# The value half of a dense expert layer with tokens as output rows, summed in PSUM over all blocks

## The reference

```python
x = x + peer(rmsnorm(x, g_ffn), ...)           # 128 x 128 experts of one neuron
#   ids, gates: for each token and 8 heads, the 16 best of 128^2 experts
#   act = gelu(h . u[ids]);  out = sum over the chosen of gates * act * v[ids]
ple_gate = sigmoid(rmsnorm(x, g_ple) @ w_ple_gate)
x = x + ple_gate * (p @ w_ple_proj)
return rmsnorm(x, g_final)
```

## Time and profile before

| | |
|---|---|
| median of 3 runs | 1931.49 us (1930.06 to 1932.35) |
| the profiled execution | 1934.96 us, its span 1933.1 us |
| mean granted TensorE clock | 0.983 |
| TensorE busy | 1854.1 us, 96% of the span |
| VectorE, ScalarE, GpSimd busy | 1271.2, 750.4, 1137.2 us |
| DMA | 360.90 MB, 187 GB/s |

### The profile page before, as it was taken

How to read it: one execution, slowest core, us unless ns; L and a number is a source line. 1 busy time by engine, 2 the same in 40 slices (tenths; PEclk the granted TensorE clock), 3 DMA queues, 4 the chain that set the end, 5 groups by cost and what they waited for, 6 DMA issues and landing times.

```text
span 1933.1 us, 24399 instructions
## 1 busy us (share of the span) xinstructions
PE 1854.1 (96%) x9045; PEld 1611.0 (83%) x9045; DVE 1271.2 (66%) x2244; ACT 750.4 (39%) x1190; POOL 1137.2 (59%) x666
## 2 busy tenths in 40 slices
...
GB/s 196 78 66 66 58 99 95 120 67 87 103 140 145 147 131 215 172 180 174 186 192 173 185 172 235 216 166 323 331 328 343 325 347 326 327 335 349 194 33 44
DMA packets 187509, 360.90 MB, mean 187 GB/s; under 512 B 17408, under 2 KB 123904, under 8 KB 185728
## 3 DMA queue, kind: packets, MB, share of 16 engines
...
## 4 chain that ended last, share of the span: by engine, by line
PE 75%; POOL 17%; issue 3%; DMA 2%; DVE 1%; ACT 1%; ACTq 0%; SPq 0%; DVEq 0%
PE bank L745 36%; PE bank L553 11%; PE bank L555 10%; PE bank L554 10%; POOL wl L492 7%; POOL picked L520 6%; PE bank L770 2%; POOL gout L527 2%; POOL rows_h L527 2%; POOL rows_ex L527 1%; DMA raw<-stream 1%; PE bank L649 1%; PE bank L669 1%; PE bank L723 1%; PE bank L639 0%
## 5 line engine op out<-in xcount | busy, mean ns | idle before, releaser
L492 POOL TENSOR_TENSOR wl<-raw,wh 128x1024 fp32r<-128x1024 f32 x298 | 737.9, 2478 | 670.3 <-ACT wh L847 668.7
L847 ACT ACTIVATE wh<-raw 128x1024 fp32r<-128x1024 f32 x338 | 356.5, 1055 | 383.7 <-PE bank L555 195.2
L553 PE MATMUL bank<-hh,wh 128*128 128x512 f32 (+1 forms) x1056 | 396.6, 376 | 30.5 <-DVE x L1400 19.2
L745 PE MATMUL bank<-hh,wh 128*128 128x512 f32 x1024 | 400.3, 391 | 0.8 <-ACT scores L1002 0.8
L745 PE MATMUL bank<-hh,wl 128*128 128x512 f32 x1024 | 400.9, 391 | 0.0
L745 PE MATMUL bank<-hl,wh 128*128 128x512 f32 x1024 | 399.6, 390 | 0.0
L555 PE MATMUL bank<-hh,wl 128*128 128x512 f32 (+1 forms) x1056 | 389.4, 369 | 0.0
L554 PE MATMUL bank<-hl,wh 128*128 128x512 f32 (+1 forms) x1056 | 389.3, 369 | 0.0
L553 PEld LDWEIGHTS bank<-hh,wh 128*128 128x128 f32 x1056 | 202.6, 192 | 60.7 <-DVE x L1400 21.5
L745 PEld LDWEIGHTS bank<-hh,wl 128*128 128x128 f32 x1024 | 192.2, 188 | 37.8
L745 PEld LDWEIGHTS bank<-hl,wh 128*128 128x128 f32 x1024 | 192.3, 188 | 36.9
...
## 6 DMA issues: line engine op xcount, KB each, us to landing
raw<-stream SPq DMA_DIRECT2D x338, 512.0 KB
score_dram<-gout ACTq DMA_DIRECT2D x128, 256.0 KB, 2.5
...
gate<-gate_dram SPq DMA_DIRECT2D x16, 1536.0 KB
score_in<-score_dram SPq DMA_DIRECT2D x128, 192.0 KB
x<-xT SPq DMA_DIRECT2D x4, 512.0 KB, 5.5
picked<-score_dram,score_at POOLq DMA_INDIRECT x128
...
```

Source lines behind the costliest of these rows:

```text
L492: nc.gpsimd.tensor_tensor(wl[:, n % SL, :], raw[:, n % RAW, :], wh[:, n % SL, :].bitcast(F32), ALU.subtract).then_inc(lo_done, 1)
L553: nc.tensor.matmul(out, ah, bh, start=start, stop=False)
L745: last = nc.tensor.matmul(psum[u % 2][:], w(weights, U_DENSE + u, c), tokens[c][:, :], start=c == 0 and which == 0, stop=c == DC - 1 and w ...
L847: nc.scalar.activation(wh[:, n % SL, :], raw[:, n % RAW, :], ACT.Copy).then_inc(hi_done, 1)
```

## The change

In the V stage the activations are stationary (128 tokens of a tile) and V rows move, 512 columns at a time: a block is 3 tiles x 2 halves of the width x 3 matmuls = 18. A unit is one block of V as it lies in DRAM. The sums of all 128 blocks stay in six PSUM banks (`pairs[1]` to `pairs[3]`, a tile each), into which x is turned first (`turn_x`: 8 matmuls with the identity, for tiles 0 to 2 in the last U blocks, for tile 3 in V block 0). `add_values` is gone. Activations lie in a ring of 8 blocks, and gelu works in two PSUM banks. The last 4 blocks are done tile by tile, so that a tile's norm can begin while the next is summed.

The sum of tile 0 begins with the turned x and lies in SBUF (`sparse_sum`), and there are 8 row buffers and a lag of 5 steps. VectorE makes two of three low halves of the V stage. In the closing stage tokens are rows: ScalarE squares a tile with a sum along the row, VectorE scales the identity by 1/rms, and TensorE turns and scales the tile by 8 matmuls with it (`turn_scaled`), twice for each tile. Gate and embeddings have tokens as output rows as well (192 and 48 matmuls of 512 columns); the embeddings are copied out of PSUM. Two gate halves of 4 tiles follow, and the closing norm and the stores go tile by tile. x, hh and hl are now single tensors. The core of the diff (new waits of the closing stage and its last functions are left out):

```diff
@@ -63,16 +62,18 @@
...
-GELU_BANKS = 3
-OUT_BANKS = 3
+LAST = 4
+RING = 8
...
-ROWS = 6
-ROW_LAG = 4
+ROWS = 8
+ROW_LAG = 5
...
-N_UNITS = U_PLE + DC + 2
+U_GATE = U_PLE + 3
+N_UNITS = U_GATE + DC
+END_ORDER = (1, 2, 0, 3)
...
@@ -132,14 +133,9 @@
...
-COPY_STEP = 119
-TURN_STEP = 121
-ADD_STEP = 122
 def low_by_dve(n):
-    return U_V0 + SL <= n < U_PLE and n % 3 == 0
+    return U_V0 + SL <= n < U_PLE and n % 3 != 0
...
@@ -271,34 +269,29 @@
...
+act_h = sb("act_h", [P, RING, DENSE], F32R, ex)
+act_l = sb("act_l", [P, RING, DENSE], F32R, ex)
+sparse_sum = sb("sparse_sum", [P, D], F32, ex)
...
+emb1 = sb("emb1", [P, TT, T], F32, pl)
+squares = sb("squares", [P, D], F32, pl)
...
+emb = [gout, emb1]
+xt = [sparse_sum[:]] + [x[:, 2 * t:2 * t + 2, :].rearrange("p a t -> p (a t)") for t in range(1, TT)]
+pairs = [ctx.enter_context(nc.psum_tensor(f"pair{b}", [P, D], F32)) for b in range(4)]
+psum = [pairs[b // 2][:, b % 2 * T:(b % 2 + 1) * T] for b in range(8)]
...
@@ -444,20 +452,28 @@
...
+        if n == U_PLE:
+            sp.dma_start(raw[:, n % RAW, :].rearrange("p (k t) -> p k t", k=2), pT).then_inc(raw_in[n % RAW], 16)
+        elif U_PLE < n < U_GATE:
+            sp.dma_start(raw[:, n % RAW, :], stream[U_PLE + 5 * (n - U_PLE - 1)]).then_inc(raw_in[n % RAW], 16)
+        elif n >= U_GATE:
+            half, kk = divmod(n - U_GATE, 4)
+            first = U_PLE + 5 * half + 1
+            part = stream[first:first + 4, :, 2 * P * kk:2 * P * (kk + 1)]
+            sp.dma_start(raw[:, n % RAW, :].rearrange("p (j w) -> p j w", j=4),
+                         part.rearrange("j p w -> p j w")).then_inc(raw_in[n % RAW], 16)
...
+    for i, tile in enumerate(END_ORDER):
+        for half in range(2):
+            k = 2 * i + half
+            sp.wait_ge(out_ready, k + 1)
+            sp.dma_start(outT[4 * half:4 * (half + 1), :, tile * P:(tile + 1) * P].rearrange("c p t -> p c t"),
+                         outb[:, k % 4, :].rearrange("p (c t) -> p c t", c=4)).then_inc(stored[k % 4], 16)
+    for i in range(4):
+        sp.wait_ge(stored[i], 32)
...
@@ -524,7 +540,7 @@
...
-        nc.gpsimd.indirect_dma_start(vrow[k % ROWS], None, row_list,
+        nc.gpsimd.indirect_dma_start(rows[:, k % ROWS, :], None, row_list,
...
@@ -782,57 +798,137 @@
...
+    def turn_x(tile, pair):
+        for c in range(DC):
+            last = nc.tensor.matmul(pairs[pair][:, c * P:(c + 1) * P], x[:, c, tile * P:(tile + 1) * P], ident[:],
+                                    start=c % 4 == 0, stop=tile == 0 and c % 4 == 3)
+        return last
...
+        if u == NK - TAIL_U + 1:
+            pe.wait_ge(quad_out, QUADS)
+            turn_x(0, 2).then_inc(x_turned, 1)
+            turn_x(1, 1)
+        elif u == NK - TAIL_U + 5:
...
+            turn_x(2, 2)
+    def block_values(b, tile):
+        at = slice((tile - 1) * P, tile * P)
+        for half in range(2):
+            cols = slice(half * T, (half + 1) * T)
+            last = three(pairs[tile][:, cols], act_h[:, b % RING, at], act_l[:, b % RING, at],
+                         wh[:, (U_V0 + b) % SL, cols], wl[:, (U_V0 + b) % SL, cols], False, b == NK - 1)
+        return last
+    for b in range(NK - LAST):
+        wait_low(pe, U_V0 + b)
+        pe.wait_ge(wsplit, b + 1)
+        for tile in range(1, TT):
+            if b == 0 and tile == TT - 1:
+                pe.wait_ge(wsplit, RING)
+                turn_x(tile, tile)
+            last = block_values(b, tile)
+        last.then_inc(unit_used, 1)
+    def turn_scaled(tile, pair):
+        for c in range(DC):
+            last = nc.tensor.matmul(pairs[pair][:, c * P:(c + 1) * P], xt[tile][:, c * P:(c + 1) * P], scaled[:, tile, :],
+                                    start=True, stop=True)
+        return last
+    def turn2(i):
+        tile = END_ORDER[i]
+        pe.wait_ge(diag2_ready, tile + 1)
+        if i >= 2:
+            pe.wait_ge(hf2_ready, 2 * (i - 1))
+        elif i == 0:
+            pe.wait_ge(wsplit, NK)
+        turn_scaled(tile, i % 2).then_inc(turned2, 1)
+    for tile in range(1, TT):
+        for b in range(NK - LAST, NK):
+            if tile == 1:
+                wait_low(pe, U_V0 + b)
+                pe.wait_ge(wsplit, b + 1)
+            last = block_values(b, tile)
+            if tile == TT - 1:
+                last.then_inc(unit_used, 1)
+            elif b == NK - 1:
+                last.then_inc(v_done, 1)
+        if tile > 1:
+            pe.wait_ge(x_copied, tile - 1)
+            turn2(tile - 2)
+    pe.wait_ge(row_added, HK)
+    turn2(2)
...
@@ -1049,71 +1145,128 @@
...
+    def act_bank(b):
+        return psum[6 + b % 2 if b < RING else b % 2][:, 0:DENSE]
...
+        if b == 0:
...
+        elif b == RING:
+            act.wait_ge(early_done, NK)
+        elif b % RING >= 2 or b > RING + 1:
+            act.wait_ge(wsplit, b - 1)
+        nc.scalar.activation(act_bank(b), score_in[:, h % SCORE_BUFS, b % SC, :], ACT.Gelu).then_inc(gelu_done, 1)
...
+        if b >= RING:
+            act.wait_ge(unit_used, U_V0 + b - RING + 1)
+        nc.scalar.activation(act_h[:, b % RING, :], act_bank(b), ACT.Copy).then_inc(wcopy, 1)
...
+        if u == NK - TAIL_U + 2:
+            act.wait_ge(x_turned, 1)
+            for par in range(2):
+                act.wait_ge(stage_out[par], 16 * (CHUNKS // 2))
+            nc.scalar.activation(sparse_sum[:], pairs[2][:], ACT.Copy).then_inc(sum_copied, 1)
...
+        if step >= -RING:
+            high_act(step + RING)
+        if -RING - 2 <= step < -2:
+            gelu(step + RING + 2)
+    gelu(RING)
+    gelu(RING + 1)
...
+        high_act(step + RING)
+        gelu(step + RING + 2)
...
+        if step < NK - RING:
+            next_high(U_V0 + step)
+    def std_of(tile):
+        if tile == 0:
...
+        else:
+            act.wait_ge(x_copied, tile)
+            act.wait_ge(squared2, tile)
+        nc.scalar.activation(squares[:], xt[tile], ACT.Square, accum_out=ssq2[:, tile:tile + 1]).then_inc(squared2, 1)
+        act.wait_ge(squared2, tile + 1)
+        nc.scalar.activation(std2[:, tile:tile + 1], ssq2[:, tile:tile + 1], ACT.Sqrt, bias=eps[:],
+                             scale=1.0 / D).then_inc(std2_ready, 1)
+    def high2(i):
+        cols = slice(END_ORDER[i] * P, (END_ORDER[i] + 1) * P)
+        for half in range(2):
+            act.wait_ge(hf2_ready, 2 * i + half + 1)
+            nc.scalar.activation(hh[:, 4 * half:4 * (half + 1), cols],
+                                 hf2[:, half, :].rearrange("p (c t) -> p c t", c=4), ACT.Copy).then_inc(hh2_ready, 1)
+    def embeddings(half):
+        for tile in range(TT):
+            i = TT * half + tile
+            act.wait_ge(emb_ready, i + 1)
+            nc.scalar.activation(emb[half][:, tile, :], psum[4 + i % 2], ACT.Copy).then_inc(emb_out, 1)
+    std_of(0)
+    for n in range(U_PLE - SL, U_PLE - LAST):
+        next_high(n)
+    std_of(1)
+    std_of(2)
+    high2(0)
+    std_of(3)
+    for n in range(U_PLE - LAST, U_PLE):
+        next_high(n)
+    high2(1)
+    high2(2)
+    embeddings(0)
+    high2(3)
+    embeddings(1)
+    act.wait_ge(emb_ready, 2 * TT)
+    for n in range(U_PLE, U_GATE):
+        high(n + SL)
...
@@ -1378,27 +1535,16 @@
...
+        nc.vector.tensor_tensor(act_l[:, b % RING, :], act_bank(b), act_h[:, b % RING, :].bitcast(F32),
+                                ALU.subtract).then_inc(wsplit, 1)
...
@@ -1409,59 +1555,115 @@
...
+            dve.wait_ge(sum_copied, 1)
...
+        nc.vector.scalar_tensor_tensor(out=sparse_sum[:], in0=rows[:, k % ROWS, :], scalar=pick_w[:, k:k + 1],
+                                       in1=sparse_sum[:], op0=ALU.mult, op1=ALU.add).then_inc(row_added, 1)
...
+    for b in range(RING):
...
+        weigh(step + RING + 1)
+        low_act(step + RING)
...
+    def copy_x(tile):
+        if tile == TT - 1:
+            dve.wait_ge(unit_used, U_PLE)
+        else:
+            dve.wait_ge(v_done, tile)
+        nc.vector.tensor_copy(xt[tile], pairs[tile][:]).then_inc(x_copied, 1)
+    def scale2(tile):
+        dve.wait_ge(std2_ready, tile + 1)
+        link(nc.vector.reciprocal(std2[:, tile:tile + 1], std2[:, tile:tile + 1]))
+        nc.vector.tensor_scalar(scaled[:, tile, :], ident[:], std2[:, tile:tile + 1], None, ALU.mult).then_inc(diag2_ready, 1)
+    def gained(bank, k, half):
+        return (bank.rearrange("p (c t) -> p c t", c=4),
+                gain[:, k, 4 * half:4 * (half + 1)].unsqueeze(2).to_broadcast([P, 4, P]))
+    def split2(i):
+        cols = slice(END_ORDER[i] * P, (END_ORDER[i] + 1) * P)
+        dve.wait_ge(turned2, i + 1)
+        for half in range(2):
+            if i >= 1:
+                dve.wait_ge(hl2_ready, 2 * (i - 1) + half + 1)
+            bank, g = gained(psum[2 * (i % 2) + half], 2, half)
+            nc.vector.tensor_tensor(hf2[:, half, :].rearrange("p (c t) -> p c t", c=4), bank, g, ALU.mult).then_inc(hf2_ready, 1)
+        for half in range(2):
+            dve.wait_ge(hh2_ready, 2 * i + half + 1)
```

(24 more changed lines are left out.)

326 lines of the change are left out of this document (145 added, 181 removed).

## The result

The changed kernel took 1908.5 us (median of 4 runs, 1903.9 to 1911.3) beside 1931.9 us of the kernel before (4 runs, 1930.1 to 1932.8): ratio 0.9878, 95% interval 0.9857 to 0.9899. The prediction was 1908. Measured twice more, as the control of the experiments, the same kernel took 1898.8 us (ratio 0.9816, 0.9788 to 0.9843) and 1899.6 us (0.9832, 0.9808 to 0.9855), while the kernel before stayed at 1933.7 and 1930.8. So the change is worth 23 us in the first measurement and 31 to 35 in the others, and the agreement with 1908 to half a microsecond is partly luck.

A forecast was written before the change was run, and what follows sets the result against it. GpSimd's queue was taken to set the pace, at 4.58 us a step. Terms +6.5, -7.8, -20.1 and -2.0 gave -23.4 us, so 1911.6 profiled, less 3.5 for the median: 1908 us, range 1870 to 1932.

The forecast's parts named there:

- Turns of x: Score tail: turning three tiles of x into the PSUM banks pushes the V stage's start by 6.5 us.
- GpSimd's steps: V stage, 98 steps of GpSimd: 4.50 us a step instead of 4.58, -7.8 us.
- the lock: V stage: VectorE instructions with two SBUF inputs delay GpSimd's gathers; 1.81 holds a step, 0.53 us each if apart.
- The finish: V stage from GpSimd's step 98 to the last V matmul: 98.2 us against 118.3, -20.1 us.
- The closing stage: After the V stage: 81.4 us against 83.4, -2.0 us, with 4.5 us of waits for the embeddings' banks.
- The profiled execution: Whole kernel: 1911.6 us forecast for the profiled execution, then 3.5 us off for the median, giving 1908.
- (a): V stage: GpSimd sets the pace at 4.4 to 4.6 us a step; 1897 to 1918 us, chance 0.50.
- (b): V stage: DMA sets the pace at about 336 GB/s; 8 us more than forecast, 1916 us, chance 0.15.
- Rival (c): V stage: TensorE sets the pace, as holds cost GpSimd less than half; 1870 us, chance 0.13.
- Rival (d): V stage: the SBUF sum makes it slower; S (us a GpSimd step) = 4.85, 1942 us, chance 0.12.
- Rival (e): V stage: gathers hold the SBUF path over their whole length; 5.16 us a step, 1973 us, chance 0.05.
- Rival (f): V stage: pace stays 4.58 us a step and TensorE gets no further ahead; 1934 us, chance 0.05.

The follow-up runs named there:

- e4: Changed kernel with each row gather fetching half the bytes, used for both halves of the sum; 1899.3 us, ratio 0.9834 to the kernel before.
- e2: Changed kernel with VectorE making all low halves of the V stage; 1902.2 us, ratio 0.9852 to the kernel before.
- e3: Changed kernel with the row sum left out: VectorE reduces each gathered row to one column (one SBUF input); 1896.1 us, ratio 0.9812 to the kernel before.
- e7: Changed kernel without the 112 score gathers inside the V loop and ScalarE's waits for them; 1902.2 us, ratio 0.9846 to the kernel before.
- e6: Changed kernel with the row sum left out (one SBUF input) and row gathers of half the bytes; 1876.2 us, ratio 0.9702 to the kernel before.
- e1: Changed kernel with VectorE making one of three V-stage low halves again, GpSimd two; 1979.3 us, ratio 1.0243 to the kernel before.

## Why the prediction was right, and where not

The first measurement's span is 26.5 us shorter; term by term, with the control's in brackets:

- **Turns of x, +6.5 predicted.** Step 0 came 8.0 us later (+6.8). Two turns take 3.49 us and the third 1.70, 5.2 for the three and not 6.5; the 2.8 us beside them (1.6) weren't traced, and 1.9 of the first measurement's are there before the V stage begins.
- **GpSimd's steps, -7.8 predicted.** -16.3 us (-24.2): 4.41 us a step (4.33), not 4.50; my bounds were 4.39 and 4.60. The excess over 3.61 + 0.03 is 0.77 us, of which 0.17 are waits for ScalarE (0.69 in the control), or 0.75 in e4 (4.39 us from step 0), where nothing else binds: 0.41 us for each of 1.81 holds. The mis-sized term is the lock's, by two errors against each other: a hold alone costs 0.70 to 0.77 us in the controls and e4, not 0.53, but 73 of 166 holds follow another, 0.80 a step where my lower bound had 0.54, and these cost next to nothing, not 0.15 us. That is the way of the lower bound, and the step came out near it (4.39), in the control 0.06 below.
- **The finish, -20.1 predicted.** 99.5 us for 118.3, -18.8 (103.2 us, -15.1). TensorE was indeed ahead of GpSimd's step 98 and ran without a gap; in the control it stands there once, 4.8 us, for a low half of VectorE.
- **The closing stage, -2.0 predicted.** +0.6 (+0.2): the wait for the embeddings' banks is 7.9 us, not 4.5, by the lock again.
- **The profiled execution, -3.5.** The sum gave 1911.6 us for the profiled execution, and 3.5 were taken off since the one of the kernel before lay that much above its median. The changed kernel's profiled execution took 1908.3, next to its median of 1908.5: the sum was 3.3 us too high and the deduction made up for it. That is luck. So is that the steps' 8.5 us beyond the forecast were partly taken back by the turns (1.5), the finish (1.3) and the closing stage (2.6).

The step that failed is the forecast's premise that one resource sets the pace, GpSimd (a), with the transfers (b) as an alternative to it. They bind together. For the 336 GB/s of (b) the prediction shows no working, but the height was right: e2, e3 and e7, with GpSimd idle for 32 to 154 us of 400, run at 335 to 346 GB/s and no faster. VectorE is not the bound in them: it waits 75 to 80 us for ScalarE, and ScalarE 84 to 109 us for weights. The 370 GB/s of a 20 us stretch was not the rate to divide by: it didn't last over a long stretch in any run. Whether the bound is the rate itself, or the time that one load takes from the release of its raw buffer (of four) to its landing, isn't told apart. A weight load lands 7.0 to 7.9 us after its issue in e2, e3 and e7 (median, 1310 to 1710 us), 6.3 us in the control, and 4.6 and 5.3 us in e4 and e6, which move fewer bytes; but the DMA share of e7 is only 0.91, and more raw buffers were not tried.

Rival (c), TensorE as the bound, is excluded for the change and reached in e6. Rival (d) decides from S = 4.74 and the kernel stands at 4.4; two holds together cost GpSimd 0.66 to 0.79 us and not 1.3. e1, which gives back the moved low halves, shows what the SBUF sum costs without them: 5.11 us a step and 1979 us. Rival (e) is excluded: it would give at least 5.16 us a step (5.24 with the row addition at its own 1.28 us), and 4.33 to 4.41 was measured. By the Trainium skill (SBUF — State Buffer, SBUF: two separate sides), the shared pair is held for the whole instruction. For a low half of GpSimd and a row addition the trace agrees, as in the 3.31 us at 1514.44; for gathers it does not, as the one under way at 1357.40 held up nothing. The Trainium skill (same page, Who interferes with whom) also infers that the writing of descriptors does not need the part of the pair that such a VectorE instruction takes. The measurement differs here as well: gathers that began inside one took 1.71 and 1.97 us for 0.95. Rival (f) is excluded by the pace.

Of the signs named, the 0.68 us, the gathers' means (1.34 and 1.12 us, forecast 1.2), the row addition's long waits, the finish and the closing stage came as said; GpSimd's steps took 432.5 us, inside 430 to 451, but not quite without waits (16.4 us). That GpSimd waits for data was named as a sign of being wrong, and it was the first hint at the second bound.
